# Decode attention over a paged cache: V's page loads go from SyncE's queue to ScalarE's, and decode's loops are written out with constant waits

## The chip, the core and the metric

One core of one Trainium2 chip runs the whole program. The metric is the device time of one execution in microseconds (us), lower is better. "The median of the runs" below is over three executions of the kernel before; one further execution was profiled, and every row shown is of that one.

## What is computed

One inference step of one layer of a decoder, for a prompt of 2048 rows and for 8 sequences that decode 8 tokens each. The change touches one part: the attention of the 8 decoding sequences over their past, which lies in a pool of cache pages.

```python
D_MODEL, SEQ, DEC_BATCH, DEC_SEQ = 1024, 2048, 8, 8
PAST_LEN, PAGE_SIZE, HEAD_DIM, N_HEADS = 8192, 128, 64, 8
...
k_past = cache_k[l][page_table].reshape(DB, n_past, N_HEADS, HEAD_DIM)
v_past = cache_v[l][page_table].reshape(DB, n_past, N_HEADS, HEAD_DIM)
lf_past = cache_logf[l][page_table].reshape(DB, n_past, N_HEADS).astype(jnp.float32)
kc_past = lf_past - lax.cumsum(lf_past, axis=1, reverse=True)
...
s = jnp.einsum('bqhd,bkhd->bhqk', q, k).astype(jnp.float32) * ATTN_SCALE
s = s + jnp.swapaxes(qc, 1, 2)[..., :, None] - jnp.swapaxes(kc, 1, 2)[..., None, :]
causal = (q_pos[:, None] >= k_pos[None, :])[None, None]
s = jnp.where(causal, s, NEG_INF)
p = jax.nn.softmax(s, axis=-1)
return jnp.einsum('bhqk,bkhd->bqhd', p.astype(v.dtype), v)
```

Each sequence has 8192 / 128 = 64 pages of K and 64 of V; a page is 128 tokens x 512 values in fp32, 256 KB. The page numbers come from `page_table` at run time, so each page's address is read into a register of the engine that issues its load.

## The kernel before

The program is a row of stages. The projection, the prompt's attention and the pooling come first; the decode stage (`stage_decode`, class `Decode`) runs from about 1480 to 2602 us of the span; what is left of decode's layer and the two feed-forward stages (prompt and sample) follow. The stages do not overlap at decode's two ends.

**Units and phases.** A unit is four pages, so a sequence has 16 units (`UN`), 128 in all. For a unit, `load_k` loads 1 MB of K into one of four buffers of `kin` (`NBUF`), VectorE turns it (`turn_k`, L1471, into `kt`, two buffers), and TensorE makes the logits (`qk`, L1569 and L1574), which ScalarE copies out (`copy_s`, L1555). A softmax needs the maximum over the whole sequence, so exponentials and the product with V follow one sequence later: ScalarE's `exp` (L1534), TensorE's `transpose_p` (L1583), VectorE's `copy_pt` (L1478) and TensorE's `pv` (L1594), which reads `vin` (four buffers of 1 MB). Phase s of the stage (s = 0 to 8) therefore handles K of sequence s and V of sequence s - 1: phase 0 has K alone, phases 1 to 7 both, phase 8 V alone. In one step of such a phase TensorE's queue holds transpose_p(u), qk(u), pv(u); ScalarE's holds exp(u), copy_s(u).

**Boundary.** After the 16 steps of a phase comes a chain of single operations that ends one sequence and starts the next: `finish_pe` and `finish_dve` (L1629, L1516 to L1522, L1634), the maximum (`maximum`, L1491 to L1500), `exp_new` (L1546) and the new tokens (L1612 to L1619).

**Who issues the loads.** SyncE issues all of them, in program order: for each unit first K of unit n, then V of the unit 16 before it. `load_k` waits until `turn_k` of four units earlier is done, `load_v` until `pv` of four units earlier is done. Before them stands `pages` (L1439): one load of the page numbers from `ids` into registers, with a few register operations and a bound check for each number: 8 numbers for a unit of phases 1 to 7, 4 in phases 0 and 8. Once per phase `load_seq` loads the next sequence's `qbd`, `vnew` and `wT` (0.26, 0.06 and 1.05 MB).

**Loops.** `run` writes each engine's decode program as loops on that engine (`fori`): an inner one over 4 turns of 4 units, and an outer one over pairs of phases 1 to 6. Waits in them compare with a value that the engine works out in registers.

Of the kernel before, what the change touches and what calls it, by code (L numbers as in the profile page):

```python
# [10 lines left out]
I32 = mybir.dt.int32  # L11
# [4 lines left out]
P = 128  # L16
# [3 lines left out]
NB, NT = 8, 8  # L20
# [12 lines left out]
NPG = 64  # L33
# [1342 lines left out]
class Decode:  # L1376
# [9 lines left out]
    def __init__(self, nc, m, io, sc, persist):  # L1386
# [12 lines left out]
        self.ids = m.sb("ids", [1, (NB + 1) * NPG * 2], I32)  # L1399
# [37 lines left out]
    def pages(self, s, u, first, count):  # L1437

        _, pages = self.nc.values_load_multi_w_load_instructions(  # L1439
            self.ids[0:1, ds(8 * (self.UN * s + u) + first, count)], engines=(mybir.EngineType.SP,),  # L1440
            min_val=0, max_val=NPOOL - 1)
        return pages

    def load_k(self, sp, s, u, buf, pages):
        sp.wait_ge(self.k_turned, self.UN * s + u + 1)
        for j in range(4):
            sp.dma_start(self.kin[:, buf, j, :], self.io["cache_k"][ds(pages[j], 1), :, :].rearrange("a t c -> (a t) c"))\
                .then_inc(self.k_in[buf], 16)

    def load_v(self, sp, s, u, buf, pages):  # L1450
        sp.wait_ge(self.pv_done, self.PARTS * s + u)
        for j in range(4):
            sp.dma_start(self.vin[j:P:4, buf, :, :],
# [74 lines left out]
    def exp(self, act, s, u, par, sp_):  # L1528

        if isinstance(u, int) and u == 0:  # L1530
            raise ValueError
# [109 lines left out]
def stage_decode(nc, io, sc, persist):  # L1641
    with ExitStack() as ctx:
# [4 lines left out]
        TURNS = d.UN // d.NBUF  # L1647

        def run(fori, k_step, v_step, boundary):


            def seq(s, i2, sp_, k, v):
                with fori(0, TURNS) as j:
                    for buf in range(d.NBUF):
                        u, par = d.NBUF * j + buf, buf % 2
                        if v:
                            v_step(0, s - 1, u, TURNS * (s - 1) + j, buf, par, 1 - sp_)
                        if k:
                            k_step(s, u, TURNS * s + j, buf, par, sp_)
                        if v:  # L1660
                            v_step(1, s - 1, u, TURNS * (s - 1) + j, buf, par, 1 - sp_)
                boundary(s, i2, sp_, k, v)

            seq(0, 0, 0, True, False)
            with fori(0, NB // 2 - 1) as i:
                seq(2 * i + 1, i, 1, True, True)
                seq(2 * i + 2, i + 1, 0, True, True)
            seq(NB - 1, NB // 2 - 1, 1, True, True)
            seq(NB, NB // 2, 0, False, True)

        @block.sync
        def _(sp):
# [3 lines left out]

            def k_step(s, u, turn, buf, par, sp_):

                if isinstance(s, int) and s == 0:
                    d.load_k(sp, s, u, buf, d.pages(s, u, 0, 4))  # L1680
                else:
                    pages = d.pages(s, u, 0, 8)
                    d.load_k(sp, s, u, buf, pages[0:4])
                    d.load_v(sp, s - 1, u, buf, pages[4:8])

            def v_step(half, s, u, turn, buf, par, sp_):

                if half == 1 and isinstance(s, int) and s == NB - 1:
                    d.load_v(sp, s, u, buf, d.pages(s + 1, u, 4, 4))

            def boundary(s, i2, sp_, k, v):
                if k and not (isinstance(s, int) and s + 1 >= NB):
                    d.load_seq(sp, s + 1, i2 + sp_, 1 - sp_)

            run(sp.Fori, k_step, v_step, boundary)

        @block.vector
        def _(dve):
# [16 lines left out]
            run(dve.Fori, lambda s, u, turn, buf, par, sp_: d.turn_k(dve, s, u, turn, buf, par), v_step, boundary)  # L1715

        @block.scalar
        def _(act):
            def v_step(half, s, u, turn, buf, par, sp_):
# [679 lines left out]
```

## Time and profile before

| | us |
|---|---|
| median of 3 executions | 4497.81 (4488.78 to 4499.96) |
| the profiled execution, its own time | 4493.22 |
| its span, first to last instruction | 4491.5 |
| mean granted TensorE clock | 0.856 of full speed |
| TensorE / VectorE / ScalarE / GpSimd busy | 79% / 47% / 30% / 13% of the span |
| DMA engines busy | 47% of the span |

The span is the profiled execution's first to last instruction; 1.7 us of its own time lie outside it. The shares are averages over stages with different limits, so the stage is read by itself in the rows further down. A step's time is read as the distance between one `turn_k` and the next, a phase's as the distance between its first `turn_k` and that of the next phase.

### The profile page before, as it was taken

The page shows a single profiled execution, that of the slowest core. Times are in us where ns is not written, and L with a number is a line of the kernel's source. Part 1 is how long each engine was busy: PE and PEld are TensorE (multiplying, and loading weights), DVE is VectorE, ACT ScalarE, POOL GpSimd, SP SyncE. Part 2 cuts the span into 40 slices and gives each one's busy share as a digit, 9 for nine tenths or more (in the row PEclk, how much of TensorE's full clock was granted, in tenths as well). Part 3 has the DMA queues.
Part 4 walks back from the last instruction along what each step waited for, and adds up shares of the span by engine and source line. Part 5 has one row for each costly group of instructions (what it writes and reads, how often), then busy time and mean ns, then how long its engine had stood idle before and what let it go on. Part 6 is the DMA issues. An engine that isn't in the chain of part 4 may idle for free. (4 is left out here: it accounts for less than half of the span.)

```text
span 4491.5 us, 63994 instructions
## 1 busy us (share of the span) xinstructions
PE 3565.5 (79%) x20532; PEld 2762.0 (61%) x20532; DVE 2127.8 (47%) x3019; ACT 1344.0 (30%) x2353; POOL 577.9 (13%) x950
## 2 busy tenths in 40 slices
PE   6999527888889566666666649999998999999696
PEld 6999316666678333333333228877876887787493
DVE  2111455666644433333333217756765775675421
ACT  2111104665521111111111114433443443444231
POOL 0000000000034000000000003312312331331210
PEclk9999768999999676666666569999999999999857
DMA  4333343213044777777777642363254236334444
GB/s 139 113 110 111 112 142 95 67 48 76 1 152 139 252 247 254 248 259 244 257 253 256 218 137 99 103 207 117 94 174 153 94 104 210 111 100 159 149 150 146
DMA packets 353593, 684.81 MB, mean 152 GB/s; under 512 B 51815, under 2 KB 135687, under 8 KB 343439
## 3 DMA queue, kind: packets, MB, share of 16 engines
q1 hardware_dynamic: 344775, 655.12, 45.1%
q10 hardware_dynamic: 5808, 17.57, 1.0%
q0 software_dynamic: 2880, 10.49, 0.6%
q8 instruction: 70, 1.15, 0.1%
q14 instruction: 60, 0.49, 0.0%
HBM read 603.24 MB, written 80.44 MB: 152 GB/s over the span
## 5 line engine op out<-in xcount | busy, mean ns | idle before, releaser
L1980 DVE TENSOR_TENSOR Fp_w_lo<-Fp_raw,Fp_w_hi 128x1024 fp32r<-128x1024 f32 x354 | 521.8, 1476 | 475.7 <-ACT Fp_w_hi L1924 475.5
L1881 PE MATMUL Fp_ps_u<-Fp_x_hi,Fp_w_hi 128*128 128x512 f32 x1408 | 553.1, 393 | 46.8 <-DVE Fp_x_lo L1989 28.3
L1471 DVE STREAM_TRANSPOSE E_kt<-E_kin 128x2048 f32<-128x2048 f32 x128 | 295.8, 2311 | 559.4 <-DMA E_kin<-cache_k 556.5
L1882 PE MATMUL Fp_ps_u<-Fp_x_lo,Fp_w_hi 128*128 128x512 f32 x1408 | 551.9, 392 | 0.0
L1883 PE MATMUL Fp_ps_u<-Fp_x_hi,Fp_w_lo 128*128 128x512 f32 x1408 | 551.5, 392 | 0.0
L1924 ACT CAST Fp_w_hi<-Fp_raw 128x1024 fp32r<-128x1024 f32 x354 | 369.5, 1044 | 343.2 <-PE Fp_ps_y L1883 307.2
L1569 PE MATMUL E_ps_s<-E_wT,E_sel 128*128 x512 | 176.9, 442 | 309.0 <-DVE E_kt L1471 307.4
L1569 PEld LDWEIGHTS E_ps_s<-E_wT,E_sel 128*128 128x128 f32 x512 | 111.0, 270 | 386.3 <-issue 385.0
L1881 PEld LDWEIGHTS Fp_ps_u<-Fp_x_hi,Fp_w_hi 128*128 128x128 f32 x1408 | 266.9, 190 | 105.8 <-issue 34.1
L1881 PE MATMUL Fp_ps_y<-Fp_w_hi,Fp_g_hi 128*128 128x512 f32 x704 | 287.9, 409 | 42.7 <-DVE Fp_w_lo L1980 30.5
L1882 PEld LDWEIGHTS Fp_ps_u<-Fp_x_lo,Fp_w_hi 128*128 128x128 f32 x1408 | 266.9, 190 | 55.6
L1883 PEld LDWEIGHTS Fp_ps_u<-Fp_x_hi,Fp_w_lo 128*128 128x128 f32 x1408 | 266.8, 190 | 55.6
L1555 ACT COPY E_logits<-E_ps_s 128x256 f32 x128 | 47.7, 373 | 816.5 <-PE E_ps_s L1574 816.5
L1883 PE MATMUL Fp_ps_y<-Fp_w_hi,Fp_g_lo 128*128 128x512 f32 x704 | 284.0, 403 | 0.0
L1882 PE MATMUL Fp_ps_y<-Fp_w_lo,Fp_g_hi 128*128 128x512 f32 x704 | 283.8, 403 | 0.0
L730 DVE TENSOR_TENSOR C_p_lo<-C_ps_t,C_p_hi 128x512 fp32r<-128x512 f32 (+1 forms) x320 | 189.5, 609 | 178.7 <-ACT C_p_hi L773 176.3
L2010 DVE SCALAR_TENSOR_TENSOR Fp_cv<-Fp_h,Fp_coef,Fp_cv 128x512 f32<-128x512 f32 x352 | 264.6, 752 | 12.4
L1945 ACT ACTIVATE Fp_h<-Fp_ps_u,Fp_coef 128x512 f32<-128x512 f32 x176 | 121.4, 690 | 490.7 <-PE Fp_ps_u L1883 490.6
L214 PE MATMUL A_ps_p<-A_w_hi,A_x_hi 128*128 128x412 f32 (+1 forms) x680 | 243.2, 358 | 25.5 <-DVE A_w_lo L326 25.5
L1574 PE MATMUL E_ps_s<-E_kt,E_qbd 128*32 128x128 f32 x4096 | 248.8, 385 | 0.0
L216 PE MATMUL A_ps_p<-A_w_hi,A_x_lo 128*128 128x412 f32 (+1 forms) x680 | 239.8, 353 | 0.0
L215 PE MATMUL A_ps_p<-A_w_lo,A_x_hi 128*128 128x412 f32 (+1 forms) x680 | 239.6, 352 | 0.0
(288 smaller groups left out, 6123.1 us busy)
## 6 DMA issues: line engine op xcount, KB each, us to landing
E_kin<-cache_k SPq DMA_DIRECT2D x512, 256.0 KB, 3.3
E_vin<-cache_v SPq DMA_DIRECT2D x512, 256.0 KB, 3.9
Fp_raw<-w_up_t SPq DMA_DIRECT2D x178, 512.0 KB, 4.0
Fp_raw<-w_down SPq DMA_DIRECT2D x176, 512.0 KB, 3.5
Fs_wu<-w_up_t SPq DMA_DIRECT2D x22, 1024.0 KB, 4.6
sc_qk<-A_qk SPq DMA_DIRECT2D x16, 1024.0 KB, 5.7
Fs_wd<-w_down SPq DMA_DIRECT2D x22, 512.0 KB, 3.7
A_prow<-w_in SPq DMA_DIRECT2D x8, 1028.0 KB, 4.9
```

Of the source, the lines that this page charges most:

```text
L214: nc.tensor.matmul(out, x_hi[:, t % 2, c, :], w_hi[:, c, cols], start=c == 0, stop=False)
L215: nc.tensor.matmul(out, x_hi[:, t % 2, c, :], w_lo[:, c, cols], start=False, stop=False)
L216: last = nc.tensor.matmul(out, x_lo[:, t % 2, c, :], w_hi[:, c, cols], start=False, stop=c == DC - 1)
L1471: self.nc.vector.transpose(self.kt[:, par, :, :].rearrange("p f (j t) -> p j f t", j=4), self.kin[:, buf, :, :].rearrange("p j (f t) -> p ...
L1569: nc.tensor.matmul(out, self.sel[:, st, :], self.wT[:, sp_, ds(u * P, P)], start=True, stop=False, skip_group_check=True)
L1574: last = nc.tensor.matmul(out[32 * hs:32 * hs + 32, :], self.qbd[:, sp_, f, :], self.kt[:, par, f, :], start=False, stop=half == 1, skip_g ...
L1881: nc.tensor.matmul(out, a_hi, b_hi, start=first, stop=False)
L1882: nc.tensor.matmul(out, a_hi, b_lo, start=False, stop=False)
L1883: return nc.tensor.matmul(out, a_lo, b_hi, start=False, stop=last)
L1924: nc.scalar.copy(w_hi[:, s, :], raw[:, q, :]).then_inc(hi_done, 1)
L1980: nc.vector.tensor_tensor(w_lo[:, s, :], raw[:, q, :], w_hi[:, s, :].bitcast(F32), ALU.subtract).then_inc(lo_done, 1)
L2010: last = nc.vector.scalar_tensor_tensor(dst, src, w, dst, ALU.mult, ALU.add)
```

## The change

- `load_v` moves from SyncE's queue to ScalarE's. ScalarE issues V of units 0 and 1 at the start of the stage, and V of unit m + 2 right behind exp(m), ahead of copy_s. Its wait is the same condition as before (pv of four units before the loaded one is done), left out where no such unit exists.
- SyncE keeps `load_k` and `load_seq`, and its loop is over K alone, through all 8 sequences. Each engine reads only its own 4 page numbers for a unit; `ids` is the table itself, not the interleaved copy that `lay_out_pages` made.
- `run` has no loops on the engines any more: all 9 phases x 16 units are written out, and every wait and buffer address is a constant.

The buffers, the sizes of the transfers, the work on TensorE and VectorE and its order are the same.

```diff
--- before.py
+++ after.py
@@ -1396,7 +1396,7 @@
         self.mx, self.mxb, self.mxe = m.sb("mx", [P, 2]), m.sb("mxb", [2, 32]), m.sb("mxe", [P, P])
         self.lp, self.rec, self.osb = m.sb("lp", [P, 2]), m.sb("rec", [P, 1]), m.sb("osb", [P, 2 * P])
         self.sel, self.lsel, self.osel = m.sb("sel", [P, 2, P]), m.sb("lsel", [P, 2, P]), m.sb("osel", [P, AC, 16])
-        self.ids = m.sb("ids", [1, (NB + 1) * NPG * 2], I32)
+        self.ids = m.sb("ids", [1, NB * NPG], I32)
         self.zero = m.sb("zero", [P, 2 * P])
         self.ps_s = m.ps("s", [P, 2, 512])
         self.ps_t = m.ps("t", [P, 512])
@@ -1434,23 +1434,27 @@
         sp.dma_start(self.wT[:, sp_, :], self.sc["wT"][ds(i2, 1), :, sp_ * 2048:(sp_ + 1) * 2048]
                      .rearrange("a p c -> (a p) c")).then_inc(self.seq_in[sp_], 16)
-    def pages(self, s, u, first, count):
-
+    def pages(self, s, u, engine):
+
+        first = 4 * (self.UN * s + u)
         _, pages = self.nc.values_load_multi_w_load_instructions(
-            self.ids[0:1, ds(8 * (self.UN * s + u) + first, count)], engines=(mybir.EngineType.SP,),
-            min_val=0, max_val=NPOOL - 1)
+            self.ids[0:1, first:first + 4], engines=(engine,), min_val=0, max_val=NPOOL - 1)
         return pages
-    def load_k(self, sp, s, u, buf, pages):
+    def load_k(self, sp, s, u):
+        buf, pages = u % self.NBUF, self.pages(s, u, mybir.EngineType.SP)
         sp.wait_ge(self.k_turned, self.UN * s + u + 1)
         for j in range(4):
             sp.dma_start(self.kin[:, buf, j, :], self.io["cache_k"][ds(pages[j], 1), :, :].rearrange("a t c -> (a t) c"))\
                 .then_inc(self.k_in[buf], 16)
-    def load_v(self, sp, s, u, buf, pages):
-        sp.wait_ge(self.pv_done, self.PARTS * s + u)
+    def load_v(self, act, s, u):
+        buf, pages = u % self.NBUF, self.pages(s, u, mybir.EngineType.Activation)
+        before = self.UN * s + u - self.NBUF
+        if before >= 0:
+            act.wait_ge(self.pv_done, 2 + self.PARTS * (before // self.UN) + 1 + before % self.UN + 1)
         for j in range(4):
-            sp.dma_start(self.vin[j:P:4, buf, :, :],
+            act.dma_start(self.vin[j:P:4, buf, :, :],
                          self.io["cache_v"][ds(pages[j], 1), :, :].rearrange("a (b t) c -> (a t) b c", b=4))\
                 .then_inc(self.v_in[buf], 16)
@@ -1527,8 +1531,6 @@
     def exp(self, act, s, u, par, sp_):
-        if isinstance(u, int) and u == 0:
-            raise ValueError
         act.wait_ge(self.t_done, self.PARTS * s + u)
         for st in range(2):
             last = self.nc.scalar.activation(self.ecur[:, par, st, :].rearrange("p (t j) -> p j t", j=4),
@@ -1645,54 +1647,31 @@
         zeroed = m.sem("zeroed")
         block = ctx.enter_context(nc.Block())
         TURNS = d.UN // d.NBUF
-
-        def run(fori, k_step, v_step, boundary):
-
-            def seq(s, i2, sp_, k, v):
-                with fori(0, TURNS) as j:
-                    for buf in range(d.NBUF):
-                        u, par = d.NBUF * j + buf, buf % 2
-                        if v:
-                            v_step(0, s - 1, u, TURNS * (s - 1) + j, buf, par, 1 - sp_)
-                        if k:
-                            k_step(s, u, TURNS * s + j, buf, par, sp_)
-                        if v:
-                            v_step(1, s - 1, u, TURNS * (s - 1) + j, buf, par, 1 - sp_)
-                boundary(s, i2, sp_, k, v)
-
-            seq(0, 0, 0, True, False)
-            with fori(0, NB // 2 - 1) as i:
-                seq(2 * i + 1, i, 1, True, True)
-                seq(2 * i + 2, i + 1, 0, True, True)
-            seq(NB - 1, NB // 2 - 1, 1, True, True)
-            seq(NB, NB // 2, 0, False, True)
+        V_AHEAD = 2
+
+        def run(k_step, v_step, boundary):
+            for s in range(NB + 1):
+                k, v, sp_ = s < NB, s > 0, s % 2
+                for u in range(d.UN):
+                    j, buf, par = u // d.NBUF, u % d.NBUF, u % 2
+                    if v:
+                        v_step(0, s - 1, u, TURNS * (s - 1) + j, buf, par, 1 - sp_)
+                    if k:
+                        k_step(s, u, TURNS * s + j, buf, par, sp_)
+                    if v:
+                        v_step(1, s - 1, u, TURNS * (s - 1) + j, buf, par, 1 - sp_)
+                boundary(s, s // 2, sp_, k, v)
         @block.sync
         def _(sp):
             d.consts(sp)
             d.load_seq(sp, 0, 0, 0)
             sp.wait_ge(d.cin, 64)
-
-            def k_step(s, u, turn, buf, par, sp_):
-
-                if isinstance(s, int) and s == 0:
-                    d.load_k(sp, s, u, buf, d.pages(s, u, 0, 4))
-                else:
-                    pages = d.pages(s, u, 0, 8)
-                    d.load_k(sp, s, u, buf, pages[0:4])
-                    d.load_v(sp, s - 1, u, buf, pages[4:8])
-
-            def v_step(half, s, u, turn, buf, par, sp_):
-
-                if half == 1 and isinstance(s, int) and s == NB - 1:
-                    d.load_v(sp, s, u, buf, d.pages(s + 1, u, 4, 4))
-
-            def boundary(s, i2, sp_, k, v):
-                if k and not (isinstance(s, int) and s + 1 >= NB):
-                    d.load_seq(sp, s + 1, i2 + sp_, 1 - sp_)
-
-            run(sp.Fori, k_step, v_step, boundary)
+            for s in range(NB):
+                for u in range(d.UN):
+                    d.load_k(sp, s, u)
+                if s + 1 < NB:
+                    d.load_seq(sp, s + 1, (s + 1) // 2, (s + 1) % 2)
         @block.vector
         def _(dve):
@@ -1712,19 +1691,25 @@
                     d.maximum(dve, s, sp_)
                     d.new_pt(dve, s)
-            run(dve.Fori, lambda s, u, turn, buf, par, sp_: d.turn_k(dve, s, u, turn, buf, par), v_step, boundary)
+            run(lambda s, u, turn, buf, par, sp_: d.turn_k(dve, s, u, turn, buf, par), v_step, boundary)
         @block.scalar
         def _(act):
+            act.wait_ge(d.cin, 64)
+            for u in range(V_AHEAD):
+                d.load_v(act, 0, u)
+
             def v_step(half, s, u, turn, buf, par, sp_):
                 if half == 0:
                     d.exp(act, s, u, par, sp_)
+                    if d.UN * s + u + V_AHEAD < d.UN * NB:
+                        d.load_v(act, s + (u + V_AHEAD) // d.UN, (u + V_AHEAD) % d.UN)
             def boundary(s, i2, sp_, k, v):
                 if k:
                     d.exp_new(act, s, sp_)
-            run(act.Fori, lambda s, u, turn, buf, par, sp_: d.copy_s(act, s, u, par, sp_), v_step, boundary)
+            run(lambda s, u, turn, buf, par, sp_: d.copy_s(act, s, u, par, sp_), v_step, boundary)
         @block.tensor
         def _(pe):
@@ -1747,7 +1732,7 @@
                         d.seq_ready(pe, s + 1, i2 + sp_, 1 - sp_)
                     d.new_tokens_pe(pe, s, sp_)
-            run(pe.Fori, lambda s, u, turn, buf, par, sp_: d.qk(pe, s, u, par, sp_), v_step, boundary)
+            run(lambda s, u, turn, buf, par, sp_: d.qk(pe, s, u, par, sp_), v_step, boundary)
@@ -2306,14 +2291,6 @@
     c["c_causal"] = np.where(r[:, None] >= r[None, :], 0.0, NEG).astype(mybir.dt.np(BF16))
     return c
-
-def lay_out_pages(table):
-
-    slots = table.reshape(NB, NPG // 4, 4)
-    keys, values = np.concatenate([slots, slots[-1:]]), np.concatenate([slots[:1], slots])
-    return np.stack([keys, values], 2).reshape(1, (NB + 1) * NPG * 2)
 def lay_out_ffn(a):
@@ -2375,7 +2352,7 @@
     arrays["cache_k"] = a["cache_k"][0].reshape(NPOOL, PAGE, AW)
     arrays["cache_v"] = a["cache_v"][0].reshape(NPOOL, PAGE, AW)
     arrays["cache_logf"] = a["cache_logf"][0].reshape(NPOOL, PAGE * H)
-    arrays["page_ids"] = lay_out_pages(a["page_table"])
+    arrays["page_ids"] = a["page_table"].reshape(1, NB * NPG)
     arrays["page_rows"] = a["page_table"].reshape(NB // 2, P).T
     arrays.update(lay_out_ffn(a))
     arrays.update(constants())
```

Where the queues' rows stand follows, at the two places that matter (`E_ids` are the page numbers; ISA and REGISTER_ALU rows are register operations, checks and waits; DMA rows are page loads). **SyncE**, before, in a phase with K and V: the four V loads of one unit, and what stands ahead of the next unit's K loads.

```order
L1451 REGISTER_ALU
L1453 ISA
L1453 DMA E_vin<-cache_v 32x4x512
L1453 ISA
L1453 DMA E_vin<-cache_v 32x4x512
L1453 ISA
L1453 DMA E_vin<-cache_v 32x4x512
L1453 ISA
L1453 DMA E_vin<-cache_v 32x4x512
L1439 ISA
L1439 TENSOR_LOAD E_ids
L1439 ISA x16
```

**SyncE** now, one whole unit of any phase.

```order
L1440 TENSOR_LOAD E_ids
L1440 ISA x8
L1448 ISA
L1448 DMA E_kin<-cache_k 128x512
L1448 ISA
L1448 DMA E_kin<-cache_k 128x512
L1448 ISA
L1448 DMA E_kin<-cache_k 128x512
L1448 ISA
L1448 DMA E_kin<-cache_k 128x512
```

Four V loads, half of the register operations and the one in front of the page numbers are gone from each unit of SyncE's queue.

**ScalarE** before, in a phase with K and V: one exp, the copy, and the next exp.

```order
L1534 ISA
L1534 REGISTER_ALU
L1534 ACTIVATE E_ecur,E_sums<-E_logits,E_nbias 128x4x32
L1534 ISA
L1534 ACTIVATE E_ecur,E_sums<-E_logits,E_nbias 128x4x32
L1554 ISA
L1555 ISA
L1555 COPY E_logits<-E_ps_s 128x2x128
L1532 ISA
```

**ScalarE** now, from one exp to the copy of the same step.

```order
L1536 ACTIVATE E_ecur,E_sums<-E_logits,E_nbias 128x4x32 x2
L1440 TENSOR_LOAD E_ids
L1440 ISA x8
L1457 ISA
L1457 DMA E_vin<-cache_v 32x4x512
L1457 ISA
L1457 DMA E_vin<-cache_v 32x4x512
L1457 ISA
L1457 DMA E_vin<-cache_v 32x4x512
L1457 ISA
L1457 DMA E_vin<-cache_v 32x4x512
L1557 COPY E_logits<-E_ps_s 128x2x128
```

The page numbers and the four V loads of unit m + 2 now stand between exp(m) and the copy of the same step, so the copy, and the exp behind it, wait until they are issued.

## Rows read from the trace of the kernel before

**Rows 1.** Stretches of decode: stretch, its length, busy time (instructions), clock, DMA share, GB/s.

```profile
core 0: us, PE busy (x) PEld busy (x) DVE busy (x) ACT busy (x) POOL busy (x), PEclk, DMA share, GB/s
1491.00:1546.00 55.00, 37.77 (x515) 24.36 (x518) 34.67 (x15) 5.22 (x14) 0.00 (x0) 0.75 0.86 287
1561.00:1680.00 119.00, 77.68 (x816) 44.67 (x816) 39.72 (x31) 17.96 (x75) 0.00 (x0) 0.70 0.76 250
1680.00:1699.00 19.00, 8.27 (x74) 4.75 (x70) 9.48 (x13) 1.89 (x9) 0.00 (x0) 0.68 0.85 293
```

**Rows 2.** Waits in decode: engine, tile, line, what it waited for, total us, times, longest.

```profile
DVE E_kt L1471 <- DMA E_kin<-cache_k: 556.5, 110, 10.7
PE E_ps_s L1569 <- DVE E_kt L1471: 307.4, 103, 20.5
PE E_ps_o L1594 <- DMA E_vin<-cache_v: 23.8, 11, 2.7
```

**Rows 3.** Waits of SyncE's queue, 1490 to 2600 us (the whole answer).

```profile
SPq L1453 <- PE E_ps_o L1619: 5.8, 1, 5.8
```

**Rows 4.** Timeline of SyncE's queue, phase 4: start, time, line, transfer, count.

```profile
2021.81 1.90 SPq L1447 DMA_DIRECT2D E_kin<-cache_k  x4
2023.96 2.98 SPq L1453 DMA_DIRECT2D E_vin<-cache_v  x4
2030.45 1.90 SPq L1447 DMA_DIRECT2D E_kin<-cache_k  x4
```

**Rows 5.** The same queue in phase 0, K alone.

```profile
1520.10 22.24 SPq L1447 DMA_DIRECT2D E_kin<-cache_k  x25
```

**Rows 6.** The same queue in phase 8, V alone.

```profile
2565.24 27.34 SPq L1453 DMA_DIRECT2D E_vin<-cache_v  x24
```

**Rows 7.** Line L1439, the page numbers: duration ns min/median/max, first and last start.

```profile
L1439 SPq TENSOR_LOAD <-E_ids x144: 295/524/542, 1483.0 to 2587.9; - x144
```

**Rows 8.** V's DMA issues, from the page: count, KB each, median us to landing.

```profile
E_vin<-cache_v SPq DMA_DIRECT2D x512, 256.0 KB, 3.9
```

**Rows 9.** Timeline of one step of phase 4, 2000 to 2025 us.

```profile
2013.52 0.79 PE L1569 MATMUL E_ps_s<-E_wT,E_sel 128*128 x2 [2.62 <-DVE E_kt L1471]
...
2016.83 1.87 PE L1594 MATMUL E_ps_o<-E_vin,E_pt 128*32 128x256 f32 x16
2017.21 0.37 ACT L1555 COPY E_logits<-E_ps_s 128x256 f32 x1 [7.27 <-PE E_ps_s L1574]
...
2017.52 0.52 ACT L1534 ACTIVATE E_ecur<-E_logits,E_nbias 128x128 f32 x1
...
2018.23 0.20 ACT L1534 ACTIVATION_READ_ACCUMULATOR E_ecur<-E_logits,E_nbias  x1
2018.63 0.44 PE L1583 MATMUL E_ps_t<-all_ident,E_ecur 128*128 128x128 f32 x2
```

**Rows 10.** Timeline across the boundary from phase 4 to 5.

```profile
2094.91 2.31 DVE L1471 STREAM_TRANSPOSE E_kt<-E_kin 128x2048 f32<-128x2048 f32 x1 [5.95 <-DMA E_kin<-cache_k]
...
2095.44 0.34 SPq L1434 DMA_DIRECT2D E_wT<-sc_wT  x1
...
2104.98 1.90 SPq L1447 DMA_DIRECT2D E_kin<-cache_k  x4
...
2116.25 2.31 DVE L1471 STREAM_TRANSPOSE E_kt<-E_kin 128x2048 f32<-128x2048 f32 x1 [0.46 <-issue]
```

**Rows 11.** VectorE's timeline: first `turn_k` of phase 1.

```profile
1561.43 2.31 DVE L1471 STREAM_TRANSPOSE E_kt<-E_kin 128x2048 f32<-128x2048 f32 x1 [0.27 <-issue]
```

**Rows 12.** VectorE's timeline: first `turn_k` of phase 7.

```profile
2392.26 2.31 DVE L1471 STREAM_TRANSPOSE E_kt<-E_kin 128x2048 f32<-128x2048 f32 x1
```

**Rows 13.** TensorE's timeline: first `pv` of phase 8.

```profile
2531.56 1.94 PE L1594 MATMUL E_ps_o<-E_vin,E_pt 128*32 128x256 f32 x16 [0.61 <-DVE E_pt L1478]
```

**Rows 14.** Timeline at decode's end: the last `pv`.

```profile
2595.79 1.94 PE L1594 MATMUL E_ps_o<-E_vin,E_pt 128*32 128x256 f32 x16 [2.50 <-DMA E_vin<-cache_v]
```

**Rows 15.** A store that ScalarE's queue issues: duration ns min/median/max.

```profile
L1154 ACTq DMA_DIRECT2D sc_x1T<-Dp_rT x16: 439/450/1392, 1292.3 to 1475.1; - x16
```

## The prediction

> **What bounds the kernel now.** The change touches only decode, so I read that stage: its stretches, then its waits, then the queue that the waits lead to.
>
> The stretches first. With K and V both flowing, the DMA engines are 76% busy at 250 GB/s and TensorE's granted clock is 0.70, a mix of its two levels, 2.4 and 1.2 GHz. With K alone, and in a boundary, they are 85 to 86% busy at 287 and 293 GB/s. No engine is full [rows 1].
>
> The waits: `turn_k` waited 556.5 us for K pages, and `qk` 307.4 us for `turn_k`; `pv` waited only 23.8 us for V [rows 2]. So K is late. Four units of K may be in flight, four steps ahead of use. If they were, a slow transfer would be the cause; but SyncE's queue, which issues them, waited 5.8 us in the whole stage [rows 3]. It is never held by a full buffer. It is simply always issuing: four K loads take 1.90 us, the four V loads 2.98, and the next unit's K starts 8.64 us after this one's [rows 4]. The rest, about 3.5 us, is the reading of 8 page numbers, of which 0.52 us is the load itself [rows 7], and the gaps between the pieces. With K alone 25 loads take 22.24 us, so a unit takes (22.24 - 0.33) / 6 = 3.65 us, 1.7 of it page numbers. With V alone 24 loads take 27.34 us, so (27.34 - 3.0) / 5 = 4.87 us a unit [rows 5, 6]; 3.65 + 4.87 = 8.52, which is the step. **Decode's step is SyncE's issue time.** Even the boundary (last `turn_k` of a phase to the first of the next, 21.3 us here [rows 10]) costs little by itself, since SyncE goes on issuing in it and the next steps use what it got ahead.
>
> Phases 1 to 7: from the first `turn_k` of phase 1 to that of phase 7 are six phases in 830.8 us, 138.5 us each [rows 11, 12].
>
> The Trainium skill speaks against the change in "DMA: Bandwidth & Descriptors", section "Issuing engines are not separate DMA queues": loads issued from several engines run on the same 16 DMA engines, and a second issuer saves only the sequencer's time, "which is usually small relative to the DMA itself". By that rule the step would stay (rival F). Here the rows differ from "usually": the sequencer's time is all of it.
>
> **The change, step by step.** A phase of the changed kernel is set by the largest of four things.
>
> 1. *SyncE.* Only K is left: 3.65 us a unit [rows 5], 58 us a phase. No longer a bound.
>
> 2. *ScalarE and the loop through TensorE.* V's issue costs 4.87 us a unit on SyncE [rows 6], less 0.15 to 0.25 for address arithmetic that constants save: I take 4.7. ScalarE's own work is the copy (0.31 us to the start of exp) and exp (start 2017.52, last accumulator end 2018.43, 0.91 us) [rows 9]. If its queue runs on under the activations the cycle is 4.7 + 0.3 + 0.4 = 5.4; if nothing overlaps, 5.9. The copy waits for `qk` anyway, and TensorE's own work is qk 3.3 us (2013.52 to 2016.83), pv 1.87 and the transpose 0.44 to 0.69, so about 5.9 us at the lower clock [rows 9]. At the higher one it is nearly half. I take 6.0. Queued behind the V loads on ScalarE are copy_s(u) and exp(u+1), for which TensorE's next `transpose_p` waits; since qk(u) ends about 5.6 us after exp(u) starts, the 4.7 us are mostly hidden under it at the lower clock, and exposed by some 2 us at the higher. The new wait on `pv_done` is for pv two steps back, already done. A phase: 15 steps x 6.0 + a boundary. The boundary was 21.3 us, in which a loop on an engine also jumps back; I take 20: 110 us.
>
> 3. *The DMA engines.* A phase moves 16 x 8 x 0.262 = 33.55 MB, plus 1.37 MB for the next sequence's tiles: 34.9 MB. Rate at full share: 250 / 0.76 = 329, 287 / 0.86 = 334, 293 / 0.85 = 345 GB/s [rows 1]; so 101 to 106 us if they never idle. The highest share seen over a long stretch is 86%, but there the issuer was the limit; with two issuers I take 95% (chosen), 111 us. In the boundary K can run only four units ahead (4.2 MB, 13 us), so they idle for some us of the 20.
>
> 4. *V two units ahead instead of four.* V(m+2) is issued 5.6 us after exp(m) starts; pv(m+2) starts two steps and about 5.1 us later (exp 0.9, transpose 0.7, qk 3.5). Slack: 2 x 6.0 - 0.5 = 11.5 us, against 3.9 us to landing [rows 8]. Costs nothing unless landing more than doubles.
>
> Bounds 2 and 3 lie at 110 and 111 and share no slack, so each step's jitter costs: I take **116 us a phase**, 22.5 less than 138.5, times 7 = -157.5.
>
> *Phase 8, V alone*, gets slower. Before, four units lay ready and SyncE fed 4.87 us a unit: first to last pv 64.2 us [rows 13, 14]. Now two are ready and ScalarE's cycle is 4.7 + 0.4 to 0.9; the load of V(15) follows exp(13): 13 x 5.1 to 5.6, + 4.7 + 3.9 = 75 to 81. So +11 to +17, taken +13.
>
> *Phase 0*: SyncE's 3.65 us a unit remains; two V units (2.1 MB) ride along in the 14% of DMA time that is free in 55 us (about 2.6 MB). 0 to +4, taken +1. Loops written out: their register work was part of the step of an engine that waited, so nothing; where the outer loop jumps back I see SyncE quiet from 2095.8 to 2105.0, against 3 us between other units [rows 10], and that is inside the 138.5.
>
> Sum: -157.5 + 13 + 1 = -143.5, so 4493.2 - 143.5 = 4349.7 for an execution like the profiled one. That one lies 4.6 us below the median of three, so **4354 us**, 3.2% faster.
>
> **The rivals.**
>
> - *A, the forecast*: ScalarE, TensorE and the DMA engines bind together, 110 to 121 us a phase: 4312 to 4389. Chance 0.50.
> - *B, the overlap is better*: with less waiting TensorE's clock rises (K alone, where TensorE waits less, shows 0.75 [rows 1]), ScalarE's queue runs under its activations, step 5.4, and the DMA engines hold 345 GB/s at full share. Phase 15 x 5.4 + 20 = 101, raised to 105 by the 101 of the DMA side: 7 x 33.5 = 234.5 less 14, about 4277. Against: all three must come together. 0.12.
> - *C, two streams do not raise the DMA rate*: it stays at the 290 GB/s of K alone. 34.9 / 0.29 = 120, + 3 for the boundary's idle time: 123, so 7 x 15.5 - 14 = 94 saved: 4403. For it: that figure is the most any long stretch shows. Against: the queue then had 14% free. 0.14.
> - *D, the two queues get in each other's way while issuing*: each V load waits for a K load's issue, 0.33 us at worst (1.90 / 4 less the gap), 1.3 us a step, so 7.3 x 15 + 20 = 129.5: 63 - 14 = 49 saved: 4449. For it: a store on ScalarE's queue usually took 0.45 us to issue, once 1.39 [rows 15]. Against: once in 16. Between this and A lies part of the chance. 0.15.
> - *E, slower*: V comes late. K may hold four units (4.2 MB) in the DMA engines; if V waits behind all of it, landing takes 4.2 / 0.329 = 12.8, + 3.2 for its own megabyte, + 1: 17 us. A step needs landing below 2c - 0.5, so c = 8.75: a phase of 15 x 8.75 + 20 = 151, 7 x 12.8 + 14 = 104 longer: 4602. It decides from the landing at which 15c + 20 reaches 138.5: c = 7.9, a landing of 15.3 us. Against: four times the landing of now. 0.06.
> - *F, no change*: the step is the transfers' own time and not their issue, so a second issuer saves nothing: about 4498. For it: `turn_k` is seen waiting for a DMA. Against: the 24% of DMA time that is free [rows 1] and a queue that never waits [rows 3]. 0.03. This is what the rule quoted above would give.
>
> On D the Trainium skill has a rule: "Perfetto Trace Analysis", section on the per-instruction lifecycle, says that an issuing sequencer locks the descriptor generator for its own use while it makes a DMA's descriptors. If that lock is shared between the two queues, its price is D's 1.3 us a step and the time 4449; the row's one 1.39 us agrees with it, the median does not show it.
>
> **How the numbers follow.** The time is A's. The range must leave out no more than 2 in 10: from 4300, which takes in the nearer part of B, to 4445, which holds C and most of D. Outside stay the far half of B, a little of D, E and F. A measurement of this kernel can tell about 0.3% (13 us) from no change. Faster: A, B, C and D, and the near part of E, 0.91. Same 0.03. Slower 0.06.
>
> **What would show each step.** SyncE's queue waits on `k_turned` for much of the stage. `turn_k` to `turn_k` about 6.4 us in the middle of a phase. ScalarE's queue solid with V's issue, four loads in about 3 us. DMA share 90% or more at 300 to 320 GB/s between about 1560 and 2370 us. `turn_k`'s wait for K falls from 556.5 us to below 150; `pv`'s wait for V stays below 100. Phase 8 takes 75 us or more. Wrong would be: V issues of 0.9 us each (D), a DMA share of 95% at 290 GB/s (C), long waits of `pv` for V (E), or a step of 5.5 (B).

## The result and the profile after

The changed kernel takes 4210.04 us (median of 4, 4204.7 to 4223.57) against 4498.59 us before on the same chips: ratio 0.9368, 95% interval 0.9342 to 0.9393. It is 6.3% faster. The forecast was 4354 us with a range from 4300 to 4445: the direction and the reason for it (SyncE's issue time) were right, the size was half of what came, and the time lies below the range.

The profiled execution's span is 4206.6 us, 284.9 less than before. Cut at the same marks as the forecast's sum, it went as follows. "Forecast" adds the terms of the sum to the column before.

| stretch | before | forecast | after |
|---|---|---|---|
| start to first `turn_k` of phase 1 [rows 11] | 1561.4 | 1562.4 | 1562.0 |
| from there to first `pv` of phase 8 [rows 13], 7 phases | 970.1 | 812.6 | 688.4 |
| first to last `pv` of phase 8 [rows 14] | 64.2 | 77.2 | 64.6 |
| rest of the span | 1895.7 | 1895.7 | 1891.6 |

The marks of the changed kernel, from VectorE's and TensorE's timelines (start, time, line, operation), one `turn_k` each of phases 1 and 7, and the first and last `pv` of phase 8:

```profile
1561.98 2.29 DVE L1475 STREAM_TRANSPOSE E_kt<-E_kin 128x2048 f32<-128x2048 f32 x1
...
2156.32 2.29 DVE L1475 STREAM_TRANSPOSE E_kt<-E_kin 128x2048 f32<-128x2048 f32 x1
...
2250.38 1.94 PE L1596 MATMUL E_ps_o<-E_vin,E_pt 128*32 128x256 f32 x16 [0.52 <-DVE E_pt L1482]
...
2314.96 1.94 PE L1596 MATMUL E_ps_o<-E_vin,E_pt 128*32 128x256 f32 x16 [0.52 <-DVE E_pt L1482]
```

Six phases in 594.3 us are 99.1 us each, where there were 138.5 and I expected 116. The seven phases hold 281.7 of the 284.9 us. All "phases" below are worked out in this way, from the first `turn_k` of phase 1 to that of phase 7, by six.

The stretch rows for one phase of the changed kernel, phase 5, in the columns of [rows 1]:

```profile
core 0: us, PE busy (x) PEld busy (x) DVE busy (x) ACT busy (x) POOL busy (x), PEclk, DMA share, GB/s
1958.00:2057.00 99.00, 66.73 (x886) 41.09 (x886) 49.07 (x43) 19.20 (x83) 0.00 (x0) 0.81 0.97 355
```

Against the 119 us of a phase's steps in [rows 1], the DMA share went from 76% to 97%, the rate from 250 to 355 GB/s, and TensorE's granted clock from 0.70 to 0.81. The same phase in 40 slices, from the DMA view, shows what the mean hides: 375 to 395 GB/s nearly throughout, and only the last two slices, the end of the boundary, and the first few of the next phase, where the loads start again, are well below.

```profile
DMA  3799999999999999999999999999999999999910
GB/s 113 247 325 379 381 386 368 384 396 386 380 387 389 385 384 388 384 387 382 387 387 384 387 392 379 389 383 374 389 378 387 389 386 394 380 387 387 359 60 0
```

The waits, decode alone; they answer to [rows 2] and [rows 3].

```profile
SPq L1448 <- DVE E_kt L1475: 219.2, 84, 19.2
```

```profile
PE E_ps_o L1596 <- DMA E_vin<-cache_v: 107.3, 66, 4.0
...
PE E_ps_s L1571 <- DVE E_kt L1475: 39.0, 14, 24.4
...
DVE E_kt L1475 <- DMA E_kin<-cache_k: 31.3, 14, 14.3
```

SyncE's queue, which waited for a buffer once before, 5.8 us, now does so 84 times, 219.2 us. `turn_k`'s wait for K fell from 556.5 to 31.3 us. `pv`'s wait for V rose from 23.8 to 107.3 us: V is only two units ahead, and its landing takes longer. The page's DMA issues show that, against 3.9 us in [rows 8]:

```profile
E_vin<-cache_v ACTq DMA_DIRECT2D x512, 256.0 KB, 9.4
E_kin<-cache_k SPq DMA_DIRECT2D x512, 256.0 KB, 9.2
```

One step of phase 4, timeline (start, time, engine, line), against [rows 9]. ACT rows are ScalarE's work, ACTq rows are what its queue issues:

```profile
1903.40 0.54 ACT L1536 ACTIVATE E_ecur<-E_logits,E_nbias 128x128 f32<-128x128 f32 x1
...
1904.64 2.92 ACTq L1457 DMA_DIRECT2D E_vin<-cache_v  x4
1907.96 0.37 ACT L1557 COPY E_logits<-E_ps_s 128x256 f32<-128x256 f32 x1 [3.63 <-issue]
1908.23 0.52 ACT L1536 ACTIVATE E_ecur<-E_logits,E_nbias 128x128 f32<-128x128 f32 x1
```

From exp to exp are 4.83 us; the `turn_k` distances in the first two thirds of a phase are mostly 4.5 to 5.0 (starts 1961.59, 1966.55 and 1971.09 in phase 5), the later ones up to 8. The mean of phase 5 is 5.0 us a step. exp starts at 1903.40 and the first V load issues at 1904.64: the page numbers were read while the activations ran.

### The profile page after: what moved, and what is told of

Read it like the earlier page. It is cut to its first block and busy times, and to the rows that moved or that the text cites. A ratio compares the mean times of both kernels' runs of the same rounds, so it can differ in the third digit from the quotient of the medians.

```text
span 4206.6 us, 61907 instructions
## 1 busy us (share of the span) xinstructions
PE 3409.6 (81%) x20532; PEld 2690.0 (64%) x20532; DVE 2128.9 (51%) x3019; ACT 1339.6 (32%) x2353; POOL 577.9 (14%) x950
## 5 line engine op out<-in xcount | busy, mean ns | idle before, releaser
L1475 DVE STREAM_TRANSPOSE E_kt<-E_kin 128x2048 f32<-128x2048 f32 x128 | 294.6, 2302 | 32.0 <-DMA E_kin<-cache_k 31.3
L1995 DVE SCALAR_TENSOR_TENSOR Fp_cv<-Fp_h,Fp_coef,Fp_cv 128x512 f32<-128x512 f32 x352 | 264.7, 752 | 12.4
L1596 PE MATMUL E_ps_o<-E_vin,E_pt 128*32 128x256 f32 x2048 | 172.9, 465 | 115.9 <-DMA E_vin<-cache_v 107.3
L2047 POOL TENSOR_TENSOR Fp_spare<-Fp_zero 128x1 f32<-128x1 f32 x352 | 138.3, 393 | 666.5 <-DVE Fp_cv L2003 418.2
L1482 DVE COPY E_pt<-E_ps_t 128x256 f32<-128x256 f32 x128 | 54.4, 425 | 332.2 <-PE E_ps_t L1585 332.2
L765 ACT ACTIVATE C_row<-C_row,C_least 128x1280 f32<-128x1280 f32 (+15 forms) x128 | 154.2, 1205 | 205.3 <-DVE C_row L718 157.6
```

Source lines behind the costliest of these rows:

```text
L1475: self.nc.vector.transpose(self.kt[:, par, :, :].rearrange("p f (j t) -> p j f t", j=4), self.kin[:, buf, :, :].rearrange("p j (f t) -> p ...
L1596: last = nc.tensor.matmul(self.ps_o[row:row + 32, 0:2 * P], self.pt[:, par, st, b, :], self.vin[:, buf, b, st * 2 * P:(st + 1) * 2 * P], s ...
L1995: last = nc.vector.scalar_tensor_tensor(dst, src, w, dst, ALU.mult, ALU.add)
```

## The experiments

Four questions: is it the split or the written-out loops; does the rate need a second queue, or only loads issued fast enough; what does V's short lead cost; what binds now. Each run is compared with the kernel before on the same chip. Code is shown against the changed kernel unless said otherwise, and only the lines that carry the point; ... marks what is left out.

**e1, one queue, loops written out.** V back on SyncE behind K, all else as changed.

```diff
-        buf, pages = u % self.NBUF, self.pages(s, u, mybir.EngineType.Activation)
+        buf, pages = u % self.NBUF, self.pages(s, u, mybir.EngineType.SP)
...
-            for s in range(NB):
+            for s in range(NB + 1):
                 for u in range(d.UN):
-                    d.load_k(sp, s, u)
+                    if s < NB:
+                        d.load_k(sp, s, u)
+                    if s > 0:
+                        d.load_v(sp, s - 1, u)
```

> The second half of the change alone: loops written out with constant waits, V still issued by SyncE behind K of the same unit. Theory 1 (decode's step is the issue time of the queue that issues; two issuers halve it): SyncE's unit is the sum of the two queues' units as the changed kernel shows them, K about 3.4 us and V about 4.2 us, so 7.6 to 7.9 us against 8.5 before; a phase 124 to 128 us, the whole 4385 to 4420 us. Theory 3 (the written-out loops bring most of the gain): 4210 to 4300 us.

Measured 4465.47 us, ratio 0.9934 (0.9915 to 0.9954). A phase is 133.6 us. SyncE's timeline in phase 3:

```profile
1890.23 3.00 SPq L1457 DMA_DIRECT2D E_vin<-cache_v  x4
1894.79 1.89 SPq L1448 DMA_DIRECT2D E_kin<-cache_k  x4
1898.24 3.25 SPq L1457 DMA_DIRECT2D E_vin<-cache_v  x4
1903.04 1.89 SPq L1448 DMA_DIRECT2D E_kin<-cache_k  x4
```

V starts are 8.01 us apart and K starts 8.25. Over phases 1 to 7 the median distance from one unit's K to the next is 8.12 us, and 8.31 before: the loops' register work was a small part of SyncE's unit, and two reads of 4 numbers (0.30 us each) take a little more than one of 8 (0.52). The rest of the gain lies in the boundaries. Before, SyncE issued no K for 14.2 and 14.4 us at the two where the outer loop jumps back, and for 8.4 to 8.7 us at the other four; here it is 7.7 to 8.4 us at all six. The expectation was some 45 to 80 us too good; what stands is that written-out loops alone bring 0.7% on one queue.

**e2, two queues, loops kept.** From the kernel before: ScalarE issues V, SyncE K alone; the loops and register waits stay, phase 8 apart.

```diff
                 if half == 0:
                     d.exp(act, s, u, par, sp_)
+                    if not (isinstance(u, int) and u + 2 >= d.UN):
+                        d.load_v(act, s, u, (buf + 2) % d.NBUF, d.pages(s, u + 2, mybir.EngineType.Activation),
+                                 d.PARTS * s + u + 2)
...
```

> The first half alone: ScalarE issues V two units ahead, SyncE keeps K, but the engines' loops and their register waits stay as before (phase 8 alone is written out). Theory 1: ScalarE's unit grows from about 4.5 by the address and wait arithmetic to 4.8 to 5.1 us, still under the 5.4 us that 2.1 MB take at 386 GB/s; 4215 to 4260 us. Theory 3: 4350 us or more.

Measured 4217.93 us, ratio 0.9384 (0.9364 to 0.9403), which overlaps the changed kernel's 0.9342 to 0.9393; a phase is 99.5 us. **The split is the gain.** Its middle steps are 5.2 to 5.6 us instead of 4.5 to 5.0, and yet the phase is the same. Its late steps stay at 5.2 to 5.7 us, where the changed kernel's reach 8, and its boundaries are 20 to 21 us. V lands in 5.4 us here, and `pv` hardly waits for it:

```profile
PE E_ps_o L1593 <- DMA E_vin<-cache_v: 3.8, 8, 0.6
```

So the 107.3 us of such waits in the changed kernel are not by themselves what its phase costs. What the two have in common is the DMA engines: about 385 GB/s through the phase and next to nothing at its end (the last slices of phase 5 here are 373, 51 and 0).

**e3 and e4, fixed pages.** The page table is left out: unit m loads pages 4m to 4m+3, so no number is read, and the attention is over other pages than it should be. e3 has all loads on SyncE, e4 is the changed kernel otherwise.

```diff
-        _, pages = self.nc.values_load_multi_w_load_instructions(
-            self.ids[0:1, first:first + 4], engines=(engine,), min_val=0, max_val=NPOOL - 1)
-        return pages
+        return [first + j for j in range(4)]
```

> Leaves out the page table: the pages loaded are fixed ones, unit m takes pages 4m to 4m+3 (other data, same bytes), so no page numbers are read. All loads on SyncE's queue, loops written out. Four K issues and four V issues take 4 x 0.38 + 4 x 0.65 = 4.1 us a unit, less than the 5.4 us of the transfers. Theory 1 (the DMA rate of before was low because too little was in flight, one queue is enough): DMA rate 370 to 390 GB/s in the phases, about 4200 to 4225 us. Theory 2 (one queue cannot pass some 330 GB/s, the second queue itself raises the rate): phases of 111 us or more, about 4300 us.

> Leaves out the page table in the same way, but with V on ScalarE's queue as in the changed kernel: the control for the one-queue run. ScalarE's unit falls to about 3.0 to 3.5 us. If the transfers are the bound of the changed kernel, the phase stays at 96 to 99 us and the time at 4185 to 4212 us; if ScalarE's 4.5 us a step is, the phases fall below 92 us and the time below 4160 us.

e3: 4132.89 us, ratio 0.919 (0.9164 to 0.9216), phase 91.8. e4: 4165.11 us, ratio 0.9263 (0.9245 to 0.9281), phase 95.8. One queue is enough, and is the faster of the two. Phase 5 of e3, the DMA view in 40 slices, all of it on one queue:

```profile
DMA  9897999999999999999999999999999999999999
GB/s 389 325 368 257 317 273 331 362 329 377 395 398 387 385 386 386 387 388 384 388 387 386 387 389 378 386 390 386 386 393 382 389 390 373 363 387 385 387 388 386
...
q1 hardware_dynamic: 17720, 33.03, 102.3%
```

386 GB/s sustained from a single queue: the second queue does not raise the rate, it takes issue time off the first. The rival that one queue could not pass some 330 GB/s is out. (A share over 100% says that the packets' recorded times add up to more than the engines' time. It is a load figure and no fraction.) e3 also beats e4 by 4.0 us a phase, though both issue fast enough. In e3 V runs up to four units ahead and is not in ScalarE's way; e8 below speaks for the lead, but these two runs don't separate the two.

**e5, one queue, real page numbers, no bound check.** From e1: 8 numbers in one read, and the check of each one dropped. The result is the full one.

```diff
-            self.ids[0:1, first:first + 4], engines=(engine,), min_val=0, max_val=NPOOL - 1)
+            self.ids[0:1, first:first + count], engines=(mybir.EngineType.SP,), min_val=0, max_val=NPOOL - 1,
+            skip_runtime_bounds_check_because="the page table holds indices of the pool by construction")
...
```

> Correct page numbers, all loads on SyncE, loops written out, 8 page numbers read at once as before, but without the bound check of each number (about 0.25 us each in the SyncE rows of the run with one queue and written-out loops). SyncE's unit: 7.98 measured there less 8 x 0.25 less one of two register loads 0.3 = 5.6 to 5.8 us. Theory 1 (issue time, then the transfers' 5.4 us a unit; a second queue isn't needed): phases 92 to 95 us, 4140 to 4175 us, faster than the changed kernel. Theory 2 (the second queue is what raises the rate): above 4210 us.

Measured 4196.77 us, ratio 0.9331 (0.9315 to 0.9346), phase 99.7. Without any second queue it equals the changed kernel or is slightly ahead of it (the intervals of the ratios just overlap); it is 269 us below e1, with nothing changed but how the page numbers are read: no checks, and one read for eight. SyncE's queue still hardly waits (14 us in all). The size was missed:

```profile
1899.78 2.35 SPq L1449 DMA_DIRECT2D E_kin<-cache_k  x4
1902.32 2.97 SPq L1458 DMA_DIRECT2D E_vin<-cache_v  x4
1906.03 1.89 SPq L1449 DMA_DIRECT2D E_kin<-cache_k  x4
1908.10 2.97 SPq L1458 DMA_DIRECT2D E_vin<-cache_v  x4
1911.81 2.74 SPq L1449 DMA_DIRECT2D E_kin<-cache_k  x4
```

K starts are 6.25 and 5.78 us apart, and later ones up to 7.6: the best is the expected one, but four K issues take anything from 1.89 to 2.74 us. Long issues are seen wherever loads take long to land: a K issue has a mean of 343 ns before, 442 in the changed kernel, 573 in e3 and 655 in e9, with K landing in 3.3, 9.2, 7.7 and 13.1 us. The mean is 382 ns here. What makes them long no run isolates.

**e6, the changed kernel without bound checks.** The same argument added to the changed kernel's read.

> The changed kernel without the bound checks. ScalarE's 4.5 us step falls to about 3.5 us, as with fixed pages. If the boundary with V two units ahead (23 us) and the transfers set the phase, it stays near the run with fixed pages and two queues, 95 us a phase: 4165 to 4180 us. If ScalarE's issue were the bound, well below 4165 us.

Measured 4177.63 us, ratio 0.93 (0.9285 to 0.9316), phase 96.7. The quick steps fall from 4.5 to 3.6 us, the phase only by 2.4 us. ScalarE's issue sets single steps, hardly the phase. Its span is 34 us shorter than the changed kernel's, and the seven phases hold 15 of them. The stretch up to phase 1, where SyncE's issue of K counts, holds 10, and phase 8, where ScalarE's issue of V does, 14; behind decode it is 5 longer.

**e7 and e8, V's lead.** One constant.

```diff
-        V_AHEAD = 2
+        V_AHEAD = 1
```

> The changed kernel with V issued one unit ahead. V(m+1) is issued by 4.2 us after exp(m) starts and needed about a step later plus 4 us, so the step cannot be shorter than V's time to landing, 9.4 us at the changed kernel's DMA load and about 4 us at half of it: 6 to 7.5 us a step, 4300 to 4400 us. If V's lead doesn't matter (landing stays short): 4215 us.

> The changed kernel with V issued three units ahead: a wait on the pv just before it now stands in ScalarE's queue ahead of the copy. If V's late landing is what makes the boundary 23 us instead of the 16.5 of the one-queue run (the last pv of a phase waits for V there), the boundary falls to 18 to 20 us and the time to 4180 to 4200 us, unless the new wait of ScalarE costs it back; if V's landing isn't the cause, 4210 us or more.

With 1: 4261.06 us, ratio 0.9493 (0.947 to 0.9517), phase 105.4. With 3: 4169.6 us, ratio 0.9282 (0.9266 to 0.9297), phase 92.1. The waits of `pv` for V with a lead of 1, and with a lead of 3:

```profile
PE E_ps_o L1596 <- DMA E_vin<-cache_v: 187.5, 103, 4.9
```

```profile
PE E_ps_o L1596 <- DMA E_vin<-cache_v: 11.1, 12, 2.2
```

187.5, 107.3 and 11.1 us for leads of 1, 2 and 3. Both had the right sign; the lead of 3 gives 10 us more than expected, and the lead of 1 costs less: V lands in 6.4 us, not 9.4, and a step averages some 5.5 us, below the 6 that I had as the least. With a lead of 3 the boundary shrank only from 22.7 to 21.5 us on average, not to 18 to 20; most of the 7 us came from the steps. Phase 4 of that run:

```profile
1838.00:1930.00 92.00, 63.51 (x886) 38.77 (x886) 49.05 (x44) 19.46 (x84) 0.00 (x0) 0.83 1.04 381
```

**e9, a lead of 3 and no bound checks.**

> V three units ahead and no bound checks together, full result. With V three ahead the phase is 92.0 us at 381 GB/s, and 34.9 MB at the 389 GB/s of the run with fixed pages on one queue take 89.8 us. If the transfers bind by now, little is left: 90 to 92 us a phase, 4150 to 4170 us. If ScalarE's 4.5 us step still binds there, 3.5 us steps bring phases below 89 us and the time below 4145 us.

Measured 4159.95 us, ratio 0.9258 (0.9245 to 0.9271), phase 92.3. ScalarE's issue got cheaper by a fifth (quick steps of 3.6 instead of 4.5 us) and the phase did not move from e8's 92.1. The last seven steps of phase 4 are 5.37 to 5.42 us: 2.10 MB by 5.4 us is 388 GB/s. The transfers bind. This is the fastest version with the full result, 1.2% ahead of the changed kernel by the ratios; its interval touches e8's.

**e10, an eighth more bytes.** One more K page for each unit, into a tile that nobody reads, though `turn_k` waits for it.

```diff
...
+        sp.dma_start(self.more[:, buf, :], self.io["cache_k"][ds(pages[0], 1), :, :].rearrange("a t c -> (a t) c"))\
+            .then_inc(self.k_in[buf], 16)
...
-        dve.wait_ge(self.k_in[buf], 64 * turn + 64)
+        dve.wait_ge(self.k_in[buf], 80 * turn + 80)
```

> The changed kernel with one more K page loaded per unit by SyncE into a buffer of its own that nobody reads (turn_k waits for it): 4.2 MB more a phase, an eighth. SyncE has time for it. If the transfers set the changed kernel's phase, it grows by 4.2 / 0.386 = 10.9 us, in phase 0 by some 10 us as well: 80 to 90 us in all, about 4290 to 4300 us. If ScalarE's issue sets it, and the DMA engines have room, less than 30 us in all.

Measured 4264.71 us, ratio 0.949 (0.9475 to 0.9504): 55 us more than the changed kernel, between the two expectations. The phase is 103.8 us, 4.7 more, where the bytes alone would be 10.9 more. So the changed kernel's phase is not full: 34.9 MB at 0.386 take 90.4 of its 99.1 us, and about 6 us of the added transfers went into the 8.7 that are left. The DMA view shows where those 8.7 us lie: in the changed kernel's phase 5 the slices at the boundary lack about 8 us of transfer at 386 GB/s. The same view of e10 and of e8 has no idle slice at the end of a phase. One more unit of V in flight (e8) takes 7 of the 8.7 us, and a fifth K load in each of the four units that may be in flight (e10) takes about 6. Both runs put more in flight ahead of the boundary and have it filled: what the changed kernel has in flight doesn't last through it, and a third unit of V is enough to mend most of that. Cheaper issue at the same lead (e6) takes 2.4 us.

## Why the prediction was half right

The term of the sum that failed is the seven phases: forecast at -157.5 us, from 138.5 to 116 us each, it measured -281.7 us, to 99.1 us each. Both bounds that were to hold the phase at 110 and 111 us were mis-sized.

**What bounded the kernel: right.** Decode's step was SyncE's issue time. e1 keeps that and keeps the time, e2 removes it and has the whole gain, e3 and e5 shorten it on one queue and gain as much or more. The rival of no change, F, is out. The rule of the Trainium skill that stood beside it ("DMA: Bandwidth & Descriptors", "Issuing engines are not separate DMA queues": a second issuer saves only sequencer time) is half met: e3 and e4 confirm that it saves nothing else, but that time was everything here. One small item of this reading is off: the prediction has "about 3.5 us" for page numbers and gaps, and its own figures leave 8.64 - 1.90 - 2.98 = 3.76.

**Bound 3, the DMA engines: mis-sized, the first failed step.** I divided a rate by its busy share (250 / 0.76, 287 / 0.86, 293 / 0.85) and called 329 to 345 GB/s the rate at full share. It measured 386 to 389. A packet of 2048 bytes, one row of a page, takes 84 ns at the median already in the kernel before, and 16 engines x 2048 / 84 ns are 390 GB/s. But in its phases 1 to 6, 2.4% of these packets take over 300 ns, and they make up 12% of the packets' time; in the changed kernel it is 0.2% and 1.3%. The busy share counts that time, though nothing more is moved in it. What makes them long was not tested; that they go with a thin stream of loads shows in e1 too, with 15%. A burst of the kernel before shows it, in a view that I read too coarsely: 7 us at the start of a boundary, 2095 to 2102 us, in 40 slices:

```profile
GB/s 375 398 421 340 339 339 339 351 316 398 375 433 351 410 398 421 234 421 246 421 281 328 281 328 468 328 339 281 234 141 0 140 94 94 47 94 94 47 47 140
```

Its first 16 slices average 375. With 386 and the chosen 95% the bound is 95 us a phase, not 111. The Trainium skill gives, in "DMA: Bandwidth & Descriptors", the section on the iDMA fabric, 408.7 GB/s for a stream of loads of 1 MiB in rows of 4 KiB from SyncE alone. This kernel's loads of 256 KB in rows of 2 KB stay at 386 to 389 in the traces; that figure is 5 to 6% above them, my division 11 to 15% below.

**Bound 2, ScalarE and the loop through TensorE: mis-sized, the second failed step.** I took 6.0 us a step, and 5.4 as the best. It was 4.5 to 5.0 where ScalarE sets it, and 5.1 on average with the late steps. Three parts: the four V loads issue in 2.92 us, as on SyncE, but page numbers are read under the activations, which I had allowed only in part; TensorE's granted clock is 0.81 over a phase where it was 0.70, so qk and pv mostly run at the level of 2.4 GHz (pv 1.07 us against 1.87 in [rows 9]); and the wait of the copy for `qk` is then short. I counted TensorE's step at the lower level. That level was read from phases in which TensorE waited for K (`qk` waits 307.4 us for `turn_k` [rows 2], and 303.8 in e1, which shows 0.69); in the other runs, with 143 us of that wait or less, the phases show 0.79 to 0.85.

**The 5 us for jitter between bounds 2 and 3**: these do not add up as I had them. A phase has quick steps at ScalarE's pace while buffers are full, then slow ones at the transfers' pace. The boundary, forecast at 20, is 20.9 to 24.6 us. V's lead is not the reason (e8, a lead of three, has 20.9 to 22.4); see below.

**V two units ahead: half right.** I priced it at nothing unless landing more than doubles. It did, from 3.9 to 9.4 us, and e8 puts the price at 7 us a phase. But the way is another than the one I had: e2 has the same lead, V lands in 5.4 us, `pv` waits 3.8 us in all, and its phase is no shorter. The price is paid in what is in flight when a phase ends. The slower rival E, V late because it waits behind K, did not come: 9.4 us of landing stays far below the 15.3 at which it decides.

**Phase 8: wrong.** Forecast 13 us longer, it is 0.4 longer. ScalarE's cycle there is mostly 4.45 us, below SyncE's 4.87 in [rows 6]. That makes up for the fewer units at hand: three quick `pv` at the start, 3.1 us apart, where there were six.

**Loops written out, taken at nothing**: nothing to see with two queues (e2 against the changed kernel), but 0.7% on one (e1), half of it in boundaries like the one of [rows 10].

**The rivals.** B named the right three things (clock up, reads under the activations, the DMA engines faster) but still capped the DMA rate at 345 GB/s, and so stopped at 4277. It also named "a step of 5.5" as a sign that the forecast is wrong, and the average step is 5.1. C is refuted by 386 GB/s. D is not seen: V's issue on ScalarE, beside K's on SyncE, has a median of 610 ns and a mean of 626, against 602 and 610 on SyncE before, where D needs 330 more. K's median is unchanged at 333 ns; its mean rose from 343 to 442, but a single queue (e3) has 573, so that is no matter of two queues. The issues of K and of V (duration ns min/median/max):

```profile
L1448 SPq DMA_DIRECT2D E_kin<-cache_k x512: 332/333/2740, 1484.5 to 2213.5; - x171
```

```profile
L1457 ACTq DMA_DIRECT2D E_vin<-cache_v x512: 609/610/1509, 1484.1 to 2309.1; - x171
```

Of the 141 us by which the span is shorter than forecast, the seven phases hold 124, phase 8 holds 13, and 4 lie behind decode, where nothing was changed. That stretch takes 1891.5 to 1901.9 us over the twelve traces, so these 4 us are nothing to explain.

**The boundary's length is no measure of the queue.** It reads 21 to 25 us in the changed kernel and mostly 16.5 in e3 and e5, which suggests that V's issue on ScalarE lengthens it. The traces say otherwise: e10 has V on ScalarE too, and 16.5 to 20.0 us. From the end of a phase's last `pv` to the next `turn_k` it is 11.2 to 12.4 us in e3, e5, e10, the changed kernel and e8 alike. What differs most is the time from the last `turn_k` to the start of the last `pv`: 4.2 to 5.7 us where that `turn_k` had waited for K (e3, e5, e10), and 7.9 to 10.2 where K lay ready and VectorE was a step ahead (the changed kernel, e8). It is time moved from the steps into the boundary.

**Open.** Why some K issues take much longer than 333 ns, and what makes some packets take over 300 ns when loads are few.

## What to carry to other kernels

A queue that issues loads and never waits was itself the bound here, whatever the consumers seemed to wait for; count what it does between two loads, register reads and bound checks too, before adding a second issuer, since dropping the checks, with loops written out, did as much on one queue as the split did. A DMA rate divided by its busy share was no ceiling: take the highest rate held through a burst, or the median time of a packet, and price a step on TensorE at the clock that it will have when its waits are gone. When the transfers have become the bound, look at what is in flight where the consumers pause: a lead of three units instead of two was worth another 0.9%.

## What the runs showed of the hardware

- One queue, SyncE's, keeps the 16 DMA engines at 386 to 389 GB/s with pages of 256 KB in rows of 2 KB (e3); two queues reach the same and no more (the changed kernel, e8). A packet of 2 KB takes 84 to 87 ns at the median.
- A load's time to landing does not follow from the DMA rate. At the median V lands in 3.9 us at 253 GB/s (phases 1 to 6 before); at 352 to 355 it is 4.4 us in e5, 5.4 in e2 and 9.4 in the changed kernel; at 379 to 382 it is 7.8 in e3, 9.4 in e8 and 13.1 in e9. Of two versions that differ in the work between issues alone, the one with less of it has the longer landing (e2 and the changed kernel; e8 and e9).
- ScalarE's queue reads registers from a tile and checks them while its activations run: in the step above the read starts at 1903.26, within the copy, and the last check is at 1904.45, 0.12 us after the activations end. Its DMA issues cost what SyncE's do: 2.92 us for four V loads against 2.98 in [rows 4].
- A bound check on a number read into a register costs its queue about 0.27 us: units of SyncE at their best are 7.98 us apart in e1 and 5.77 in e5, which is 2.2 us for eight checks, with 0.07 of it for the second read. They were a quarter of SyncE's unit before.
